# Attention in a decoder step: page numbers kept in registers, four slots for the near masks, and another way to spread the inverse sums

## The chip, the cores and the metric

The kernel runs on one core of one Trainium2 chip. The metric is the time of one execution on the device in microseconds (us). The runs shown of the kernel before took 3438.68, 3438.88 and 3434.42 us, with a median of 3438.68 us. The profile comes from one more execution.

A core has five engines that run instructions of their own queues in order: TensorE (PE, matrix products), VectorE (DVE), ScalarE (ACT), GpSimd (POOL) and SyncE (SP, which here only starts transfers). They wait for each other on semaphores.

## The reference

One inference step of a small decoder with two layers (`DEPTH = 2`): layer 0 has sparse attention (8 heads of 64) and retention side by side, layer 1 a Mamba-2 mixer, and each has an MLP behind it. There are two groups of tokens: a prompt of 1024 tokens, and 8 samples of one token each, with a past of 1024 tokens in pages of 128. The change lies in layer 0's attention.

```python
def sparse_attend(q, kg, vg, idx, tpos, rel_bias):
    dist = tpos[None, :, None] - idx
    bias = jnp.moveaxis(rel_bias[t5_bucket(dist)], -1, 2).astype(jnp.float32)
    logits = jnp.einsum('bqhd,bqkhd->bqhk', q, kg).astype(jnp.float32) * (DH_A ** -0.5) + bias
    logits = jnp.where((dist >= 0)[:, :, None, :], logits, -jnp.inf)
    p = jax.nn.softmax(logits, axis=-1).astype(vg.dtype)
    return jnp.einsum('bqhk,bqkhd->bqhd', p, vg)

# prompt: for each block of QBLK = 128 queries
idx = indexer_topk(iqb, iwb, ik, tpos, k_sel)            # 256 of the keys so far
att = sparse_attend(qb, k[bi, idx], v[bi, idx], idx, tpos, rel_bias)

# samples (even_mixer_sample): keys and values are looked up in pages
page = page_table[bi, pidx // PAGE_SIZE]                 # (8 samples, 8 pages each)
kg = jnp.where(in_past, ck[page, off], k[bi, nidx])
vg = jnp.where(in_past, cv[page, off], v[bi, nidx])
att = sparse_attend(q, kg, vg, idx, pos, rel_bias)
```

## The kernel before

Layer 0's mixer is a sequence of stages. In the profiled execution they are: projection of the tokens and choice of the 256 keys (to about 485 us), the samples' softmax and the storing of k and v (485 to 514), attention of the prompt together with the samples' weighing of values (514 to 708, the function `attend`), and retention. A stage begins when all engines are done with the one before.

**Attention.** The prompt is handled in 8 blocks `i` of 128 queries. Block `i` sees the first `L = (i + 1) * 128` keys. Within a block the 8 heads `h` follow each other, so there are 64 steps `n`. Not chosen and future keys are masked: `scores` holds 1 for them, which `scale_mask` (L1841, POOL) turns into a large negative number. The relative bias matters only for the last 256 keys; POOL adds it to the mask's last 256 columns in `near_mask` (L1851), once for each step, into one of two slots. For one head:

1. PE: `dot_pair` (L1881 to L1893) computes the logits of a pair of heads `q`, 64 rows each, in pieces of 512 columns, into PSUM banks 0 to 3. Before the pair it waits until DVE has read all logits of the pair before (`s_log`).
2. DVE: the far part (L1955) adds the mask to all but the last 256 columns, the near part (L1960) adds the near mask to those; both also give the row maximum. They signal `s_far` and `s_log`. The far part exists from block 2 on. Both wait for the near mask of their step.
3. ACT: the exponential, with its row sum (`s_prob`).
4. PE: transposes of the probabilities, 128 columns each, into PSUM banks 4 and 5 in turn (L1903, `s_turned`), which ACT copies to SBUF (L2004, `s_pt`).
5. PE: the values of a pair weighed with the transposed probabilities into bank 6 (L1915).

For each block, once, the sums must divide the result. Bank 6 holds attention with head and head size on rows (four groups of 128) and queries on columns, while the sums have queries on rows. So:

1. DVE `inverse`: reciprocals `rden` of the 8 row sums (128 x 8).
2. POOL `inverse_rows` (L1856): copies each reciprocal to 64 columns, into `att` (128 x 512), at the second head of the next block.
3. PE `spread_inverse` (L1924): four transposes of that, waited for with `s_rows`, after the second head's own transposes.
4. ACT copies the result to `spread`; DVE `scale_rows` (L1973) multiplies bank 6 with it into `att`.
5. ACT rounds `att` to a high part (L2016, at head 4), and POOL `low` (L1861, at head 5) subtracts it from `att`, which gives the low part. Both go to the output projection, which works with high and low parts.

**Samples.** The values of 8 samples lie in 64 pages of 256 KB. They come in 16 halves `m` of four pages, into a ring of 6 halves (`place`): two in the weight buffers `w_loaded_sb` and `w_high_sb`, four in unused parts of `act_high_sb` and `act_low_sb`. `values_pe` weighs two halves after each of the first two pairs and one after each of the next twelve, each after a wait for its pages (L1516). ACT starts halves 0 to 2, SP the others: halves 3 and 4 in the stage before, among the stores of k and v, and the rest at the head of `attend`, followed by retention's first loads. A half is loaded by `load_pages` (L1331 to L1336):

```python
with eng.Fori(0, self.HALF) as j:
    page = eng.value_load(self.B.pages[0:1, bass.ds(j + m * self.HALF, 1)], min_val=0, max_val=NPOOL - 1)
    eng.dma_start(place[:, bass.ds(j, 1), :],
                  self.B.i[cache][0][bass.ds(page, 1)]...).then_inc(sem, 16)
```

This is a loop of the engine with four passes: it reads the page's number from the table in SBUF into a register (L1334) and starts one transfer (L1335). The key pages are loaded in the same way during the projection, by SP, on whose queue the projection's weights stand as well; POOL multiplies them with the queries (L1368) and DVE sums the products (L1374).

The order of the work is written out by hand: each engine's instructions stand in the order of its function's loops, and nothing else sets it.

## Time and profile before

| | us |
|---|---|
| runs shown: median (lowest to highest) | 3438.68 (3434.42 to 3438.88) |
| profiled execution, its own time | 3435.92 |
| profiled execution, span | 3434.4 |
| PE busy in the span | 3250.5 (95%) |
| DVE, ACT, POOL busy in the span | 1527.5, 1143.6, 1210.8 |
| attention stage | 514 to 708.4 |

The span is the time from the first to the last instruction of the profile; the execution's own time is 1.5 us longer. Attention is 5.7% of the span. PE runs at one of two clock levels, 1.2 and 2.4 GHz; the granted clock of a stretch is given as a share of full speed, so that 0.50 is all of it at the lower level and 1.00 all of it at the higher. In timelines a bracket at a row's end gives the idle time of the engine before it and the engine, tile and line that ended it; `SPq` is SP's own queue, where no computing takes place. In this profile the span's start is zero.

### The profile page before, as it was taken

How to read it: one execution, taken by the hardware profiler on the slowest of the kernel's cores; microseconds unless marked ns; L12 is line 12 of the kernel's file. 1: busy time of each engine (PE TensorE's matmuls, PEld its weight loads, DVE VectorE, ACT ScalarE, POOL GpSimd, SP SyncE). 2: the span in 40 equal slices, each digit the busy share in tenths (PEclk: the TensorE clock that was granted, in tenths of full speed). 3: DMA queues.
4: the chain of work that ended last, by engine and by line, in shares of the span. 5: the costliest groups of instructions: out<-in, count | busy, mean ns of one | idle time of the engine just before them, and what ended most of it. 6: DMA issues, size and time to landing. Idle time of an engine off the chain costs nothing. (4 is left out here: it accounts for less than half of the span.)

```text
span 3434.4 us, 57106 instructions
## 1 busy us (share of the span) xinstructions
PE 3250.5 (95%) x20508; PEld 3062.1 (89%) x20508; DVE 1527.5 (44%) x2685; ACT 1143.6 (33%) x2133; POOL 1210.8 (35%) x898
## 2 busy tenths in 40 slices
PE   7889988888999999999999999999899999999998
PEld 7569974567999999999899999998889999999998
DVE  3799983523221212122556777667742212122122
ACT  3512214532321313132445554545542312222122
POOL 2206844411322221213355555666453221212222
PEclk9989988968999999999999999999999999999999
DMA  4218646022311111112222322222431111111111
GB/s 135 54 31 139 195 172 194 18 79 88 45 49 43 49 45 47 49 43 75 61 84 80 100 94 91 82 86 70 150 134 47 49 44 48 49 43 49 43 49 68
DMA packets 344005, 263.87 MB, mean 77 GB/s; under 512 B 52134, under 2 KB 308150, under 8 KB 341910
## 3 DMA queue, kind: packets, MB, share of 16 engines
q1 hardware_dynamic: 327926, 232.18, 23.2%
q0 software_dynamic: 8192, 19.13, 1.6%
q10 hardware_dynamic: 7776, 11.09, 1.5%
q8 instruction: 68, 1.11, 0.1%
q14 instruction: 43, 0.35, 0.0%
HBM read 219.43 MB, written 44.76 MB: 77 GB/s over the span
## 5 line engine op out<-in xcount | busy, mean ns | idle before, releaser
L234 POOL TENSOR_TENSOR w_low_sb<-w_loaded_sb,w_high_sb 128x1024 fp32r<-128x1024 f32 (+1 forms) x278 | 567.9, 2050 | 1551.3 <-ACT w_high_sb L226 1533.4
L252 PE MATMUL psum<-act_high_sb,w_high_sb 128*128 128x344 f32 (+1 forms) x2400 | 769.4, 321 | 10.0 <-PEq L985 4.0
L252 PE MATMUL psum<-act_low_sb,w_high_sb 128*128 128x344 f32 (+1 forms) x2400 | 767.7, 320 | 0.0
L252 PE MATMUL psum<-act_high_sb,w_low_sb 128*128 128x344 f32 (+1 forms) x2400 | 767.5, 320 | 0.0
L252 PE MATMUL psum<-second_high_sb,w_high_sb 128*128 128x344 f32 x1728 | 553.3, 320 | 0.5 <-PEq L2369 0.5
L252 PE MATMUL psum<-second_low_sb,w_high_sb 128*128 128x344 f32 x1728 | 551.9, 319 | 0.0
L252 PE MATMUL psum<-second_high_sb,w_low_sb 128*128 128x344 f32 x1728 | 551.9, 319 | 0.0
L252 PEld LDWEIGHTS psum<-act_high_sb,w_high_sb 128*128 128x128 f32 (+1 forms) x2400 | 450.5, 188 | 11.3 <-issue 10.0
L252 PEld LDWEIGHTS psum<-act_high_sb,w_low_sb 128*128 128x128 f32 (+1 forms) x2400 | 451.0, 188 | 0.4
L252 PEld LDWEIGHTS psum<-act_low_sb,w_high_sb 128*128 128x128 f32 (+1 forms) x2400 | 450.6, 188 | 0.3
L226 ACT CAST w_high_sb<-w_loaded_sb 128x1024 fp32r<-128x1024 f32 (+1 forms) x230 | 239.5, 1043 | 523.1 <-PE psum L252 496.2
L2970 PE MATMUL psum<-act_high_sb,w_high_sb 128*128 128x344 f32 x1104 | 369.1, 334 | 12.5 <-POOL w_low_sb L234 10.7
L756 DVE TENSOR_TENSOR x_sb<-x_sb,psum 128x344 f32 (+1 forms) x192 | 98.4, 513 | 600.7 <-PE psum L252 600.7
L2970 PE MATMUL psum<-act_high_sb,w_low_sb 128*128 128x344 f32 x1104 | 354.0, 321 | 0.0
L2970 PE MATMUL psum<-act_low_sb,w_high_sb 128*128 128x344 f32 x1104 | 353.7, 320 | 0.0
L252 PEld LDWEIGHTS psum<-second_high_sb,w_high_sb 128*128 128x128 f32 x1728 | 324.5, 188 | 0.8 <-issue 0.8
L252 PEld LDWEIGHTS psum<-second_high_sb,w_low_sb 128*128 128x128 f32 x1728 | 324.8, 188 | 0.0
L252 PEld LDWEIGHTS psum<-second_low_sb,w_high_sb 128*128 128x128 f32 x1728 | 324.5, 188 | 0.0
L688 ACT ACTIVATE relu_square_sb<-relu_sb 128x344 f32<-128x344 f32 x192 | 94.5, 492 | 448.0 <-DVE relu_sb L741 448.0
L741 DVE SCALAR_TENSOR_TENSOR relu_sb<-psum,rstd_sb 128x344 f32<-128x344 f32 x192 | 99.2, 516 | 295.5 <-PE psum L252 271.0
L2970 PEld LDWEIGHTS psum<-act_high_sb,w_high_sb 128*128 128x128 f32 x1104 | 208.9, 189 | 23.0 <-issue 21.9
L2970 PEld LDWEIGHTS psum<-act_low_sb,w_high_sb 128*128 128x128 f32 x1104 | 208.7, 189 | 2.6 <-issue 1.7
(441 smaller groups left out, 4828.9 us busy)
## 6 DMA issues: line engine op xcount, KB each, us to landing
w_loaded_sb<-in_w_up SPq DMA_DIRECT2D x64, 512.0 KB, 4.1
w_loaded_sb<-in_w_down SPq DMA_DIRECT2D x64, 512.0 KB, 4.2
w_loaded_sb<-in_w_in_odd SPq DMA_DIRECT2D x48, 512.0 KB, 3.9
key_pages_sb<-in_cache_k SPq DMA_DIRECT2D x64, 256.0 KB, 2.8
ecay_sum_spread_sb<-decay_sum_scratch SPq DMA_DIRECT2D x8, 2048.0 KB, 9.8
w_loaded_sb<-in_w_in_even SPq DMA_DIRECT2D x28, 512.0 KB, 4.0
gated_scratch<-gated_sb POOLq DMA_DIRECT2D x8, 1032.0 KB, 4.4
ample_ssm_state_sb<-in_state_ssm SPq DMA_DIRECT2D x64, 128.0 KB, 6.9
```

What stands on the lines that cost most here:

```text
L226: self.nc.scalar.copy(self.wh[:, par, :, 0:width], self.wf[:, par, :, 0:width]).then_inc(self.s_w_high, 1)
L234: ins = self.nc.gpsimd.tensor_tensor(self.wl[:, par, k, 0:width], self.wf[:, par, k, 0:width], self.wh[:, par, k, 0:width].bitcast(F32), A ...
L252: ins = nc.tensor.matmul(out, w[:, par, k, 0:width], a[:, k, cols], start=n == 0, stop=n == 3 * KT - 1)
L688: nc.scalar.activation(self.sq[:, s, :], self.relu[:, s, :], ACT.Square).then_inc(self.s_square, 1)
L741: nc.vector.scalar_tensor_tensor(out=self.relu[:, s, :], in0=B.tile(self.par(e), t), scalar=0.0, in1=self.norm.rstd[:, tcols(t)], op0=ALU.max,
L756: nc.vector.tensor_tensor(xs, xs, B.tile(self.par(e), t), ALU.add).then_inc(B.s_tile_free, 1)
L2970: ins = nc.tensor.matmul(B.psum[:, t, 0:TT], w[:, par(e), k, :], a[:, k, tcols(t)], start=m == 0, stop=m == 3 * KT - 1)
```

## The change

The change has five parts.

1. **Page numbers.** `load_pages` is written out as four steps in place of the engine's loop. A new function `number` reads the table; on SP the number of a page from the 20th on is kept in a register of its own after its first read, which is that for the key page, and the value page's load uses the register (44 registers). The places of the ring become tensors of their own at the same addresses.
2. **Near masks and low part.** There are four slots for near masks, so POOL waits for the near part four steps before (not two). The low part of block `i - 1` moves from head 5 to head 7 of block `i`. The last block's low part goes from POOL to DVE.
3. **Spread by products.** POOL's `inverse_rows` goes. PE multiplies each head's reciprocals, read 64 times over as the 64 columns of the stationary side, with the unit matrix: eight products, each giving 64 rows of 128 queries. PE waits for DVE's reciprocals directly. As `att` is no longer used for the copy, DVE's `scale_rows` now waits for POOL's low part of the block before (`s_lo`), and the next reciprocals wait until PE is done with the last ones.
4. **First 512 columns early.** In blocks 5 to 7 and for all pairs of a block but the first, the products of the first 512 columns wait for the far part of the pair before, in place of its near part (`s_far` counts heads from block 2 on, so the number waited for is `2 * q - 2 * HA`). Those of the other columns wait as before.
5. The tensor `inverse_rows_or_att_sb` is called `att_sb`, and the new slots may reach 2048 bytes into `sample_mask_bias_sb`, which was last used in the stage before.

```diff
--- before.py
+++ after.py
@@ -1286,6 +1286,7 @@
+    KEPT = 20
 
...
@@ -1330,10 +1336,18 @@
 
     def load_pages(self, eng, cache, place, m, sem):
 
-        with eng.Fori(0, self.HALF) as j:
-            page = eng.value_load(self.B.pages[0:1, bass.ds(j + m * self.HALF, 1)], min_val=0, max_val=NPOOL - 1)
-            eng.dma_start(place[:, bass.ds(j, 1), :],
+        for j in range(self.HALF):
+            page = self.number(eng, m * self.HALF + j)
+            eng.dma_start(place[:, j:j + 1, :],
                           self.B.i[cache][0][bass.ds(page, 1)].rearrange("o p h d -> p o (h d)")).then_inc(sem, 16)
+
+    def number(self, eng, p):
+
+        if eng is not self.B.nc.sync or p < self.KEPT:
+            return eng.value_load(self.B.pages[0:1, p:p + 1], min_val=0, max_val=NPOOL - 1)
+        if p not in self.kept:
+            self.kept[p] = eng.value_load(self.B.pages[0:1, p:p + 1], min_val=0, max_val=NPOOL - 1)
+        return self.kept[p]
 
@@ -1776,21 +1783,23 @@
...
+    NEAR = 4
     first = B.take("first_blocks_mask_sb", [P, 2 * P])
-    near = B.take("near_mask_sb", [P, 2, 2 * P])
+    near = B.take("near_mask_sb", [P, NEAR, 2 * P])
+
-    att = B.take("inverse_rows_or_att_sb", [P, 512])
+    att = B.take("att_sb", [P, 512])
-    assert B.top <= (B.end - 6400) // 64 * 64, B.top
+    assert B.top <= (B.end - 6400) // 64 * 64 + 4 * NS * PAGES * HA, B.top
...
@@ -1846,15 +1855,10 @@
                 w = min(L, 2 * P)
                 if h == 0:
                     pool.wait_ge(s_mask, max(2, i + 1))
-                if n >= 2:
-                    pool.wait_ge(s_log, n - 1)
-                nc.gpsimd.tensor_tensor(near[:, n % 2, 0:w], mask(i)[:, L - w:L], B.bias[:, h, 2 * P - w:2 * P],
+                if n >= NEAR:
+                    pool.wait_ge(s_log, n - NEAR + 1)
+                nc.gpsimd.tensor_tensor(near[:, n % NEAR, 0:w], mask(i)[:, L - w:L], B.bias[:, h, 2 * P - w:2 * P],
                                         ALU.add).then_inc(s_near, 1)
-
-            def inverse_rows(i):
-                pool.wait_ge(s_rden, i + 1)
-                nc.gpsimd.tensor_copy(att[:].rearrange("p (h d) -> p h d", h=HA),
-                                      rden[:].unsqueeze(2).to_broadcast([P, HA, DH])).then_inc(s_rows, 1)
 
@@ -1866,26 +1870,28 @@
             for n in range(N):
                 i, h = seq[n]
                 near_mask(n)
-                if h == 1 and i >= 1:
-                    inverse_rows(i - 1)
                 if h == 3 and 1 <= i < NBLK - 1:
                     scale_mask(i + 1)
-                if h == 5 and i >= 1:
+                if h == HA - 1 and i >= 1:
                     low(i - 1)
-            inverse_rows(NBLK - 1)
-            low(NBLK - 1)
 
         @block.tensor
         def _(pe):
             def dot_pair(q):
                 i = seq[2 * q][0]
                 L = width(i)
+                early = L - 2 * P >= 512 and q % PAIRS
                 if q >= 1:
-                    pe.wait_ge(s_log, 2 * q)
+                    if early:
+                        pe.wait_ge(s_far, 2 * q - 2 * HA)
+                    else:
+                        pe.wait_ge(s_log, 2 * q)
                 if i == 4 and q % PAIRS == 0:
                     pe.wait_ge(smp.s_colk, NS - 1)
                 for c in range(0, L, 512):
                     w = min(512, L - c)
+                    if c and early:
+                        pe.wait_ge(s_log, 2 * q)
                     for e in range(2):
                         h = seq[2 * q + e][1]
                         r = slice(64 * e, 64 * e + 64)
@@ -1918,10 +1924,12 @@
 
             def spread_inverse(i):
                 k = spread_place[i]
-                pe.wait_ge(s_rows, i + 1)
+                pe.wait_ge(s_rden, i + 1)
                 pe.wait_ge(s_pt, k - 1)
-                for j in range(4):
-                    ins = nc.tensor.transpose(B.psum[:, turn_bank(k), j * P:(j + 1) * P], att[:, j * P:(j + 1) * P], B.ident[:])
+                for h in range(HA):
+                    e, c = 64 * (h % 2), h // 2 * P
+                    ins = nc.tensor.matmul(B.psum[e:e + 64, turn_bank(k), c:c + P],
+                                           rden[:, h:h + 1].to_broadcast([P, DH]), B.ident[:], start=True, stop=True)
                 ins.then_inc(s_turned, 1)
 
             dot_pair(0)
@@ -1957,19 +1965,21 @@
                                                    accum_out=mx[:, n % 3, 0:1]).then_inc(s_far, 1)
                     dve.wait_ge(s_far, n + 1 - 2 * HA)
                     start = mx[:, n % 3, 0:1]
-                nc.vector.tensor_tensor_reduce(out=logit[:, n % 3, far:L], in0=ps[:, far:L], in1=near[:, n % 2, 0:w],
+                nc.vector.tensor_tensor_reduce(out=logit[:, n % 3, far:L], in0=ps[:, far:L], in1=near[:, n % NEAR, 0:w],
                                                scale=-DH ** -0.5, scalar=start, op0=ALU.add, op1=ALU.min,
                                                accum_out=mx[:, n % 3, 1:2]).then_inc(s_log, 1)
 
             def inverse(i):
                 dve.wait_ge(s_prob, HA * (i + 1))
                 if i >= 1:
-                    dve.wait_ge(s_rows, i)
+                    dve.wait_ge(s_turned, spread_place[i - 1] + 1)
                 nc.vector.reciprocal(rden[:], total[:, i % 2, :]).then_inc(s_rden, 1)
 
             def scale_rows(i):
                 dve.wait_ge(s_pv, PAIRS * (i + 1))
                 dve.wait_ge(s_pt, spread_place[i] + 1)
+                if i >= 1:
+                    dve.wait_ge(s_lo, i)
                 nc.vector.tensor_tensor(att[:], B.psum[:, OUT, :], spread[:], ALU.mult).then_inc(s_o, 1)
 
             for n in range(N):
@@ -1983,6 +1993,9 @@
                     rotary.dve(dve, n // 2)
             inverse(NBLK - 1)
             scale_rows(NBLK - 1)
+            dve.wait_ge(s_hi, NBLK)
+            nc.vector.tensor_tensor(B.hl[:, 0:4, SEQ - P:SEQ], att[:].rearrange("p (k c) -> p k c", k=4),
+                                    B.hh[:, 0:4, SEQ - P:SEQ].bitcast(F32), ALU.subtract).then_inc(s_lo, 1)
 
         @block.scalar
         def _(act):
```

How this moves instructions, in three places. First SP's queue, at the first half of value pages in `attend` (`ISA` are register and address steps), before:

```order
L1333 UNCONDITIONAL_BRANCH [waits value_pages_weighed_118]
L1333 ISA
L1334 TENSOR_LOAD page_table_sb_338
L1334 ISA x2
L1335 ISA
L1335 DMA act_high_sb_57<-in_cache_v 128x512
L1333 REGISTER_ALU
L1333 COMPARE_AND_BRANCH
L1738 DMA rotated_sb<-retention_scratch 128x4x1032 [waits value_pages_weighed_118]
```

and after, where this is one half and the start of the next:

```order
L1341 ISA [waits value_pages_weighed_118]
L1341 DMA value_pages_sb<-in_cache_v 128x512
L1341 ISA
L1341 DMA value_pages_sb<-in_cache_v 128x512
L1341 ISA
L1341 DMA value_pages_sb<-in_cache_v 128x512
L1341 ISA
L1341 DMA value_pages_sb<-in_cache_v 128x512
L1341 ISA [waits value_pages_weighed_118]
```

The branch, the loop's step and the read of the table are gone, and a page has two instructions.

Then POOL's queue in the last two blocks (L1851 and L1860 are the near masks, L1841 and L1850 the scaling of the next block's mask, L1856 the copy of the reciprocals, L1861 and L1865 the low part), before:

```order
L1841 TENSOR_SCALAR scores_sb_343<-scores_sb_343 128x1024
L1851 TENSOR_TENSOR near_mask_sb_3978<-scores_sb_343,bias_sb_3524 128x256 [waits logits_177] x2
L1861 TENSOR_TENSOR act_low_sb_58<-inverse_rows_or_att_sb_3982,act_high_sb_57 128x4x128 [waits att_high_185]
L1851 TENSOR_TENSOR near_mask_sb_3978<-scores_sb_343,bias_sb_3524 128x256 [waits logits_177] x2
L1851 TENSOR_TENSOR near_mask_sb_3978<-scores_sb_343,bias_sb_3524 128x256 [waits logits_177,mask_scaled_173]
L1851 TENSOR_TENSOR near_mask_sb_3978<-scores_sb_343,bias_sb_3524 128x256 [waits logits_177]
L1856 COPY inverse_rows_or_att_sb_3982<-prob_sum_inverse_sb_3981 128x512 [waits sum_inverse_182]
L1851 TENSOR_TENSOR near_mask_sb_3978<-scores_sb_343,bias_sb_3524 128x256 [waits logits_177] x4
L1861 TENSOR_TENSOR act_low_sb_58<-inverse_rows_or_att_sb_3982,act_high_sb_57 128x4x128 [waits att_high_185]
L1851 TENSOR_TENSOR near_mask_sb_3978<-scores_sb_343,bias_sb_3524 128x256 [waits logits_177] x2
L1856 COPY inverse_rows_or_att_sb_3982<-prob_sum_inverse_sb_3981 128x512 [waits sum_inverse_182]
```

and after:

```order
L1860 TENSOR_TENSOR near_mask_sb_4445<-scores_sb_343,bias_sb_3880 128x256 [waits logits_177,mask_scaled_173]
L1860 TENSOR_TENSOR near_mask_sb_4445<-scores_sb_343,bias_sb_3880 128x256 [waits logits_177] x3
L1850 TENSOR_SCALAR scores_sb_343<-scores_sb_343 128x1024
L1860 TENSOR_TENSOR near_mask_sb_4445<-scores_sb_343,bias_sb_3880 128x256 [waits logits_177] x4
L1865 TENSOR_TENSOR act_low_sb_58<-att_sb_4449,act_high_sb_57 128x4x128 [waits att_high_184]
L1860 TENSOR_TENSOR near_mask_sb_4445<-scores_sb_343,bias_sb_3880 128x256 [waits logits_177,mask_scaled_173]
L1860 TENSOR_TENSOR near_mask_sb_4445<-scores_sb_343,bias_sb_3880 128x256 [waits logits_177] x7
L1865 TENSOR_TENSOR act_low_sb_58<-att_sb_4449,act_high_sb_57 128x4x128 [waits att_high_184]
```

The copies are gone, and the low part stands behind all eight near masks of a block; the last one is no longer on POOL.

Last PE's queue in block 7, around the spread of block 6 and the pair behind it (L1903 and L1909 are transposes, L1892 and L1898 the logit products), before:

```order
L1903 MATMUL psum<-ident_sb_49,qkv_sb_1841 128x128 [waits probs_copied_180,probs_178]
L1903 MATMUL psum<-ident_sb_49,qkv_sb_1841 128x128 x3
L1903 MATMUL psum<-ident_sb_49,qkv_sb_1841 128x128 [waits probs_copied_180]
L1903 MATMUL psum<-ident_sb_49,qkv_sb_1841 128x128 x3
L1924 MATMUL psum<-ident_sb_49,inverse_rows_or_att_sb_3982 128x128 [waits probs_copied_180,inverse_rows_183]
L1924 MATMUL psum<-ident_sb_49,inverse_rows_or_att_sb_3982 128x128 x3
L1892 MATMUL psum<-qkv_sb_1841 128x512 [waits logits_177]
L1892 MATMUL psum<-qkv_sb_1841 128x512 x3
L1903 MATMUL psum<-ident_sb_49,qkv_sb_1841 128x128 [waits probs_copied_180,probs_178]
L1903 MATMUL psum<-ident_sb_49,qkv_sb_1841 128x128 x3
```

and after:

```order
L1909 MATMUL psum<-ident_sb_49,qkv_sb_1841 128x128 [waits probs_copied_180,probs_178]
L1909 MATMUL psum<-ident_sb_49,qkv_sb_1841 128x128 x3
L1909 MATMUL psum<-ident_sb_49,qkv_sb_1841 128x128 [waits probs_copied_180]
L1909 MATMUL psum<-ident_sb_49,qkv_sb_1841 128x128 x3
L1931 MATMUL psum<-ident_sb_49,prob_sum_inverse_sb_4448 64x128 [waits probs_copied_180,sum_inverse_182]
L1931 MATMUL psum<-ident_sb_49,prob_sum_inverse_sb_4448 64x128 x7
L1898 MATMUL psum<-qkv_sb_1841 128x512 [waits far_logits_176]
L1898 MATMUL psum<-qkv_sb_1841 128x512
L1898 MATMUL psum<-qkv_sb_1841 128x512 [waits logits_177]
L1898 MATMUL psum<-qkv_sb_1841 128x512
L1909 MATMUL psum<-ident_sb_49,qkv_sb_1841 128x128 [waits probs_copied_180,probs_178]
L1909 MATMUL psum<-ident_sb_49,qkv_sb_1841 128x128 x3
```

The pair's four products fall into two that wait for the far logits and two that wait for all, and the spread has eight products of 64 x 128 where it had four of 128 x 128.

## Rows read from the trace of the kernel before

**Rows 1.** Window: us; PE, PEld, DVE, ACT, POOL busy; PE clock, DMA share, GB/s.
```profile
514.00:708.40 194.40, 160.67 (x1281) 99.82 (x1281) 84.68 (x272) 101.33 (x241) 77.32 (x88) 0.90 0.37 107
```

**Rows 2.** Waits in that stage: us in total, times, longest us.
```profile
DVE qkv_sb L1955 <- POOL near_mask_sb L1851: 21.2, 6, 3.7
...
PE psum L1516 <- DMA act_high_sb<-in_cache_v: 3.3, 2, 1.9
...
PE psum L1516 <- DMA w_high_sb<-in_cache_v: 2.6, 1, 2.6
...
PE psum L1516 <- DMA w_loaded_sb<-in_cache_v: 1.0, 1, 1.0
```

**Rows 3.** SP's queue, timeline: start us, us, value-page loads.
```profile
522.37 4.79 SPq L1335 DMA_DIRECT2D w_loaded_sb<-in_cache_v  x4
528.27 4.79 SPq L1335 DMA_DIRECT2D w_high_sb<-in_cache_v  x4
```

**Rows 4.** SP, one instruction: ns min/median/max, first and last start.
```profile
L1334 SPq TENSOR_LOAD <-page_table_sb x116: 262/268/1092, 283.1 to 581.0; - x116
...
L1335 SPq DMA_DIRECT2D act_low_sb<-in_cache_v x16: 345/351/390, 501.3 to 557.8; - x16
```

**Rows 5.** Windows, columns as Rows 1: one clean pair, three slow stretches.
```profile
558.12:562.71 4.59, 4.59 (x39) 2.69 (x39) 2.11 (x10) 3.38 (x9) 1.48 (x2) 1.00 0.69 181
...
543.40:558.00 14.60, 12.75 (x66) 6.35 (x62) 3.67 (x19) 4.11 (x11) 4.20 (x5) 0.65 0.65 172
...
571.00:582.00 11.00, 9.08 (x52) 5.56 (x52) 0.93 (x4) 2.67 (x7) 3.25 (x4) 0.69 0.61 166
...
653.80:660.00 6.20, 6.14 (x31) 3.70 (x33) 3.36 (x9) 2.78 (x5) 1.65 (x1) 0.54 0.00 0
```

**Rows 6.** DVE, timeline: far part of head 6, block 4.
```profile
613.58 0.56 DVE L1955 CUSTOM_DVE_ANT_0 qkv_sb<-psum,scores_sb 128x384 f32<-128x384 f32 x1 [3.65 <-POOL near_mask_sb L1851]
```

**Rows 7.** PE, timeline: the products around four waits behind DVE or ACT.
```profile
610.08 1.35 PE L1892 MATMUL psum<-qkv_sb 64*128 64x512 f32 x8
...
615.73 1.56 PE L1892 MATMUL psum<-qkv_sb 64*128 64x512 f32 x8 [1.67 <-DVE minus_row_max_sb L1960]
...
640.16 1.77 PE L1892 MATMUL psum<-qkv_sb 64*128 64x512 f32 x8 [1.28 <-DVE minus_row_max_sb L1960]
...
667.93 1.99 PE L1892 MATMUL psum<-qkv_sb 64*128 64x512 f32 x8 [0.90 <-DVE minus_row_max_sb L1960]
...
697.32 1.06 PE L1903 MATMUL psum<-ident_sb,qkv_sb 128*128 128x128 f32 x8 [0.93 <-ACT probs_turned_sb L2004]
```

**Rows 8.** PE, timeline, block 7: spread, late products, weighing of values.
```profile
679.45 0.63 PE L1924 MATMUL psum<-ident_sb,erse_rows_or_att_sb 128*128 128x128 f32 x4 [0.39 <-ACT qkv_sb L2004]
682.95 3.36 PE L1892 MATMUL psum<-qkv_sb 64*128 64x512 f32 x8 [2.87 <-DVE minus_row_max_sb L1960]
...
693.39 1.97 PE L1915 MATMUL psum<-probs_turned_sb,v_rows_sb 128*64 128x128 f32 x32
```

**Rows 9.** DVE, timeline: far part and near part of head 3, block 7.
```profile
681.41 0.95 DVE L1955 CUSTOM_DVE_ANT_0 qkv_sb<-psum,scores_sb 128x768 f32<-128x768 f32 x1
...
682.40 0.48 DVE L1960 CUSTOM_DVE_ANT_0 qkv_sb<-psum,near_mask_sb,minus_row_max_sb 128x256 f32<-128x256 f32 x1
```

**Rows 10.** POOL, timeline: the last low part.
```profile
706.78 1.26 POOL L1861 TENSOR_TENSOR act_low_sb<-erse_rows_or_att_sb,act_high_sb 128x512 fp32r<-128x512 f32 x1 [7.07 <-ACT act_high_sb L2016]
```

**Rows 11.** SP's queue, timeline: the stage's last load.
```profile
698.00 0.39 SPq L1746 DMA_DIRECT2D halves_or_values_sb<-retention_scratch  x1
```

**Rows 12.** DVE, timeline: two sums of the projection, a k copy.
```profile
299.97 1.22 DVE L1374 TENSOR_REDUCE sample_logits_sb<-key_pages_sb 128x32 f32<-128x1024 f32 x1 [4.48 <-POOL key_pages_sb L1368]
...
483.39 1.22 DVE L1374 TENSOR_REDUCE sample_logits_sb<-key_pages_sb 128x32 f32<-128x1024 f32 x1
...
497.35 0.69 DVE L1707 COPY k_rows_sb<-psum 128x512 f32<-128x512 f32 x1 [0.92 <-DMA out_k_prompt<-k_rows_sb]
```

**Rows 13.** PE, timeline: projection products behind a weight's low part.
```profile
302.32 0.42 PE L252 MATMUL psum<-act_high_sb,w_high_sb 128*128 128x344 f32 x1 [2.27 <-POOL w_low_sb L234]
```

More of the change, by code:

```diff
@@ L1323, in take_ring @@
         B = self.B
+        self.kept = {}
+        slots = [B.w_base + 4 * 2 * KT * P * a for a in range(2)]
+        slots += [base + 4 * (4 * TOK + a * self.HALF * 512) for base in (B.act_base, B.hl_base) for a in range(2)]
+        self.slots = [B.nc.alloc_sbuf_tensor_at(f"value_pages_{r}_sb", [P, self.HALF, 512], F32, offset=o)
+                      for r, o in enumerate(slots)]
         self.kp = B.take("key_pages_sb", [P, self.KRING, self.HALF, 512])
@@ L1479, in place @@
     def place(self, m):
-        B, r = self.B, m % self.VRING
-        if r < 2:
-            a = (B.wf[:], B.wh[:].bitcast(F32))[r]
-            return a.rearrange("p a k m -> p (a k m)").rearrange("p (j c) -> p j c", c=512)
-        a = (B.hh, B.hl)[(r - 2) // 2][:, 4:8, :].bitcast(F32).rearrange("p k c -> p (k c)")
-        c0 = (r - 2) % 2 * self.HALF * 512
-        return a[:, c0:c0 + self.HALF * 512].rearrange("p (j c) -> p j c", c=512)
+        return self.slots[m % self.VRING][:]
     def load_values(self, eng, m):
@@ L1790, in attend @@
     OUT = 6
-    (s_mask, s_near, s_dot, s_far, s_log, s_prob, s_turned, s_pt, s_pv, s_rden, s_rows, s_o, s_hi, s_lo) = (
+    (s_mask, s_near, s_dot, s_far, s_log, s_prob, s_turned, s_pt, s_pv, s_rden, s_o, s_hi, s_lo) = (
         B.sem(x) for x in ("mask_scaled", "near_mask", "logit_products", "far_logits", "logits", "probs", "probs_turned",
-                           "probs_copied", "values_weighted", "sum_inverse", "inverse_rows", "att", "att_high", "att_low"))
+                           "probs_copied", "values_weighted", "sum_inverse", "att", "att_high", "att_low"))
     width = lambda i: (i + 1) * P
```

## The prediction

> **What bounds the kernel now.** I read the windows first, stage by stage, then the waits of the stage that the change is in, then that stage's timelines on SP, PE, DVE and POOL. Outside attention PE sets the pace; over 194.4 us of attention it is busy for 160.7 us, at a mean clock of 0.90, and no other engine is busier than 101 us [rows 1]. So PE is the nearest thing to a bound there, and what can be won is its idle time (194.4 - 160.7 = 33.7 us) and the time lost at the lower of its two clock levels. The reader should look for who releases PE, not for who is busy. Three sorts of release matter. PE waits three kinds of value pages [rows 2]. DVE waits POOL's near masks and, one wait later, PE waits DVE [rows 2, 6, 7]. And once a block DVE waits for the spread inverse, and PE for DVE [rows 8].
>
> **Value pages (page numbers in registers).** SP starts a half of four pages every 5.90 us (528.27 - 522.37) although the four starts take 4.79 us and one DMA instruction 0.35 us; the rest is the table read (0.27 us), register work and the loop [rows 3, 4]. A pair of heads with a half in it and no such wait took PE 4.59 us, from its first product to the next pair's [rows 5], so SP falls behind and PE waits 3.3 + 2.6 + 1.0 = 6.9 us [rows 2]. The stall is paid twice. In the two stretches around these waits the granted clock is 0.65 and 0.69, that is most of the time at the 1.2 GHz level, each after PE had stood idle. PE is busy 12.75 of 14.60 us and 9.08 of 11.00 us there; at the mean clock, busy time lost against full speed is 12.75 x 0.35 + 9.08 x 0.31 = 4.5 + 2.8 = 7.3 us [rows 5]. In the new order a half that the ring has room for is four pairs of a register step and a DMA instruction, some 4 x 0.5 = 2 us, well under 4.6. What is late next: the transfers. At 0.65 of the engines' time they moved 172 GB/s, so 265 GB/s at all of it, and a half of 1.05 MB takes 4.0 us; that is under 4.6 us too, but not by much, and the ring is six halves deep. PE's wait for the spread in block 2 grows back by an estimated 0.8 us, since the slow clock had covered it. I take 6.9 + 7.3 - 0.8 = 13.4 us gained. Bounds: 0 (transfers keep the old pace) to 14.2.
>
> The Trainium skill (DMA: Bandwidth & Descriptors, "Bandwidth") gives 341 GB/s for a transfer of 1 MB and 425 at best: by that a half would take 3.1 us, and the term would be the same. The row's 265 GB/s is what I use.
>
> **Near masks and low part.** Before, POOL's low part of block i-1 stands two near masks before the end of block i and waits for ACT's high part, which comes late; DVE then waits for near mask 6, 3.65 us in block 4 [rows 6]. PE had the products of that head done at 610.08 + 1.35 = 611.43, so DVE could have started 2.1 us earlier [rows 6, 7]. With four slots the masks are made up to four heads ahead, and the low part stands behind all eight, with the whole of the next pair to hide in. PE's idle time behind this is 1.67, 1.28, 0.90 us in blocks 4 to 6 and 0.93 us in block 7 (there by way of ACT): 4.8 us gained [rows 7]. In blocks 1 to 3 the same wait cost PE nothing that a row shows. Each price is limited by PE's idle time, not by DVE's 3.65 us, because PE's own queue is late next. Bounds 2 to 5. The new wait that this brings, scaling the rows of block i only after the low part of block i-1, is met half a block before. The added wait in POOL's queue has eight mask starts behind it and none is due.
>
> **Spread by products.** The copy on POOL (once per block) goes; PE waited for ACT's copies, not for it [rows 8], so this gives nothing. Four transposes, 0.63 us, become eight fp32 products with 64 columns of weights, and these come two per product: 16 records. The nearest row is the weighing of values, same shape (128 x 64 by 128), 32 records in 1.97 us [rows 8]. With an estimated 0.27 us for the last one to end it is (1.97 - 0.27) / 32 = 0.053 us each. 16 x 0.053 + 0.27 = 1.12 us, so +0.49 us, eight times, on the chain that ends with DVE's scaling: a loss of 3.9 us. Low bound 0.2 us each; high bound, if the two column halves don't run side by side and each record takes twice as long, 16 x 0.107 + 0.27 = 1.98, +1.35 us each or 10.8 us.
>
> One rule speaks against it: the Trainium skill (TensorEngine Tiling (Array Packing), "Key Properties") says that changing the tiling mode drains the engine, and the products change it where transposes did not. The rows show such a change without a visible gap, since weighing follows transposes at once; a drain is at most the 0.27 us of one product's end, so the sum would be 2.2 us worse by the rule at its full price.
>
> **First 512 columns early.** In blocks 5 to 7 three pairs of four may begin when the far part of the head before is done. It matters where PE waits for DVE, which is the pair after the spread: the far part ends at 681.41 + 0.95 = 682.36 and the near part at 682.89 [rows 9], and PE starts at 682.95 after 2.87 us idle [rows 8]. The first two products of about 0.5 us each cover the near part, so the pair is done 0.53 us earlier: 3 x 0.53 = 1.6 us. Bounds 0 to 1.6; elsewhere PE comes late to the wait and nothing is gained.
>
> **End of the stage.** The last low part goes from POOL, 1.26 us [rows 10], to DVE, where the nearest operation on 512 columns (the k copy) takes 0.69 us [rows 12]: 0.6 us gained. SP's last load, 2 MB, is started at 698.00 [rows 11] and at the 265 GB/s above lands some 8 us later, at 706, and the new chain still ends after it: old end 706.78 + 1.26 = 708.04, less 0.6, plus the spread's 0.5. The load, 2 us ahead of it, is what would be late next.
>
> **Before attention.** The loop goes for all pages, but the table is still read once for each. Of a page's 4.79 / 4 = 1.20 us, 0.27 is the read, 0.35 the DMA instruction, and 0.58 register work and loop [rows 3, 4]; I take a quarter of that, 0.15 us, for the loop. In projection DVE waited 4.48 us for the first key half, PE 2.27 us for a weight that SP had queued behind these keys, and DVE's last sum there ends at 484.61 with nothing to wait for, so the stage ends with DVE's chain [rows 12, 13]. The first four pages then start 0.6 us earlier, and as much again without the entry into the loop (the longest table read took 1.09 us against 0.27 [rows 4]): I take 1.3 us off both waits (0 to 2.3). In the stage after it SP's k stores stand behind a half of value pages, and DVE waits 0.92 us and once again about half as long for them: 0.8 us (0 to 1.2) [rows 12]. The register copies on SP cost nothing that anyone waits for.
>
> **The sum.** 13.4 + 4.8 + 1.6 + 0.6 + 1.3 + 0.8 - 3.9 = 18.6 us. The profiled execution took 3435.92 us (its span 3434.4 and 1.5 around it), 2.8 us below the median of the runs shown, 3438.68. From its own time the sum gives 3417.3; from the median 3420.1. I forecast 3419, between them and nearer to the median.
>
> **Rivals.**
> - The clock stays low. The stalls go, but one or both stretches at the lower level come back behind other waits (the spread leaves over 1.4 us of idle time in a block): 7.3 us less, 3426. For it: in block 7 the level falls behind a spread wait alone, which stays, and 653.8 to 660 has 0.54 [rows 5]. Against it: 558 to 571 would run as now without a stall. 0.20.
> - The clock gains. The spread waits of blocks 5 to 7 get shorter by 0.5 us and the low stretches behind them vanish. One of them costs 6.14 x 0.46 = 2.8 us [rows 5]; three together an estimated 6: 3413. The idle time is still over 2 us, so 0.12.
> - Transfers bind. The pages land no faster than in the old rows (4 us a half at best against pairs of 4.6): 13.4 us less, 5.2 gained, 3432. 0.07.
> - The masks don't do what they are for: POOL, which waits for s_log and ACT as before, delivers them at the same moment, and the early columns find nothing idle. 6.4 us less, 3425. The order speaks against it. 0.06.
> - Slower: the spread. If its products go one by one and each record pays its full latency and an unhidden weight load, as much as the 3.36 / 8 = 0.42 us that a record of 512 columns took at the lower level [rows 8], it takes 16 x 0.42 = 6.7 us, +6.1 us eight times, 49 us against the 3.9 in the sum: 3464. The change turns slower once a spread takes over 0.63 + 22.5 / 8 = 3.4 us. The weighing of values shows an eighth of that price per record, so 0.03.
> - The forecast itself: 0.52.
>
> **Range and chances.** 3410 to 3430 takes in the clock either way, the masks' failure, and the spread up to its high bound (+6.9 us); transfers bound and the slower case lie outside. What a measurement can tell from no change is 0.2%, 6.9 us: same is 3432 to 3446. Transfers bound falls on its edge. Faster 0.90, same 0.07, slower 0.03.
>
> **What would show it.** Value-page DMAs of a half 2 us long in SP's timeline, no wait of PE for them, and a clock near 1.00 from 543 to 582. No wait of DVE for near masks but the first. A spread of about 1.1 us. PE's idle time in blocks 4 to 7 down to the spread waits. Attention some 16.5 us shorter and the stages before it some 2. It is wrong if attention gives back less than 10 us, if retention behind it changes by over 2 us, or if a spread takes over 1.5 us.

## The result and the profile after

| | before | changed |
|---|---|---|
| runs beside each other, median | 3438.68 us | 3418.99 us |
| profiled execution, own time | 3435.92 us | 3418.30 us |
| span | 3434.4 us | 3416.5 us |
| attention, first product to retention's first product | 514.12 to 708.40 | 514.53 to 690.97 |

The changed kernel takes 0.9949 of the time before, 95% interval 0.9937 to 0.9961: 19.7 us between the medians and 17.6 between the profiled executions. The forecast was 3419 us.

Windows of the changed kernel, columns as [rows 1]: attention, then block 2, block 3 (each from its first logit product to the next block's), and the time in which SP starts its last 44 value pages.

```profile
514.53:690.97 176.44, 156.10 (x1376) 99.32 (x1377) 85.25 (x273) 101.38 (x241) 71.05 (x79) 0.94 0.36 118
543.76:561.78 18.02, 16.82 (x147) 8.98 (x143) 8.07 (x38) 9.43 (x26) 8.87 (x12) 1.00 0.40 139
561.78:581.53 19.75, 18.41 (x162) 10.57 (x158) 8.71 (x38) 10.42 (x25) 8.12 (x10) 1.00 0.14 45
514.60:549.10 34.50, 32.22 (x235) 15.45 (x235) 10.85 (x52) 14.40 (x54) 17.92 (x27) 0.88 1.01 352
```

The same stretches of the kernel before, which [rows 5] showed only in part:

```profile
514.12:708.40 194.28, 160.67 (x1281) 99.80 (x1281) 84.68 (x272) 101.33 (x241) 77.29 (x88) 0.90 0.37 107
543.42:567.42 24.00, 20.99 (x135) 10.75 (x131) 8.07 (x38) 9.66 (x26) 9.02 (x11) 0.79 0.65 177
567.42:592.74 25.32, 21.11 (x150) 12.24 (x147) 8.69 (x38) 10.25 (x24) 8.75 (x11) 0.87 0.53 151
```

Attention is 17.84 us shorter, and 5.98 + 5.57 = 11.55 us of it lie in blocks 2 and 3. Their clock is 1.00, with 0.79 and 0.87 before. From the starts of the blocks in PE's timeline, the rest is 1.30, 1.51, 0.79 and 1.97 us in blocks 4 to 7, 0.65 us behind the last spread, and 0.07 us in blocks 0 and 1. One of the stalls that went, 1.91 us, lay in block 1 (PE's timeline before, 542.42), but the clock was low for longer at the stage's start.

The waits in attention, answering to [rows 2]; those of PE for value pages have no row any more.

```profile
PE psum L1898 <- DVE minus_row_max_sb L1968: 7.3, 5, 2.5
PE psum L1898 <- DVE minus_row_max_sb L1963: 6.6, 3, 2.3
...
DVE qkv_sb L1968 <- POOL near_mask_sb L1860: 3.9, 1, 3.9
```

Only the first near mask is waited for (21.2 us in six waits before for the far parts, [rows 2]). Of PE's waits behind DVE those behind the spread are left; three are now ended by a far part (L1963). In block 7 the timelines of PE and DVE show this, answering to [rows 8 to 10]:

```profile
664.65 1.09 PE L1931 MATMUL psum<-ident_sb,prob_sum_inverse_sb 128*64 128x128 f32 x16 [0.38 <-ACT qkv_sb L2017]
668.08 1.99 PE L1898 MATMUL psum<-qkv_sb 64*128 64x512 f32 x8 [2.33 <-DVE minus_row_max_sb L1963]
```
```profile
667.06 0.95 DVE L1963 CUSTOM_DVE_ANT_0 qkv_sb<-psum,scores_sb 128x768 f32<-128x768 f32 x1
...
668.06 0.48 DVE L1968 CUSTOM_DVE_ANT_0 qkv_sb<-psum,near_mask_sb,minus_row_max_sb 128x256 f32<-128x256 f32 x1
...
689.96 0.69 DVE L1997 TENSOR_TENSOR act_low_sb<-att_sb,act_high_sb 128x512 fp32r<-128x512 f32 x1 [0.68 <-ACT act_high_sb L2029]
```

The spread has 16 records in 1.09 us (forecast 1.12), the products start as the far part ends, 0.54 us earlier than in [rows 8], and the last low part takes DVE 0.69 us (forecast 0.69). The eight products of the pair run at full clock here, 1.99 us and not 3.36.

SP's queue: the first key half, the 44 value pages of attention and one half of them alone, answering to [rows 3]; then SP's waits in that time, and the window 520 to 540.

```profile
283.29 3.67 SPq L1341 DMA_DIRECT2D key_pages_sb<-in_cache_k  x4
...
514.61 34.46 SPq L1341 DMA_DIRECT2D value_pages_sb<-in_cache_v  x44
...
529.46 1.91 SPq L1341 DMA_DIRECT2D value_pages_sb<-in_cache_v  x4
```
```profile
SPq L1341 <- PE psum L1523: 8.2, 6, 2.0
```
```profile
520.00:540.00 20.00, 19.18 (x152) 8.74 (x144) 6.32 (x27) 8.23 (x31) 6.92 (x10) 0.92 1.05 383
```

With a table read a half's four starts take 3.67 us, not 4.79 (loop). Without reads they take 1.91 us, and the next half can follow after 2.1 us, as forecast. All 44 pages take longer, 34.46 / 11 = 3.1 us a half, because SP waits 8.2 us of that time for PE to free a place in the ring. The DMA engines are full there, with a share of 1.05 at 383 GB/s, which gives 2.7 us a half (1.05 MB / 383). Both are under the 4.6 us that PE needs.

In the stage before attention, DVE's first copy and its waits for k stores:

```profile
484.82 0.68 DVE L1714 COPY sample_qkv_rows_sb<-psum 8x512 f32<-8x512 f32 x1 [1.24 <-PE psum L1694]
...
497.63 0.69 DVE L1714 COPY k_rows_sb<-psum 128x512 f32<-128x512 f32 x1 [1.89 <-DMA out_k_prompt<-k_rows_sb]
498.98 0.69 DVE L1714 COPY k_rows_sb<-psum 128x512 f32<-128x512 f32 x1 [0.66 <-DMA out_k_prompt<-k_rows_sb]
500.30 0.69 DVE L1714 COPY k_rows_sb<-psum 128x512 f32<-128x512 f32 x1 [0.63 <-DMA out_k_prompt<-k_rows_sb]
```

The first copy stood at 485.85 before, so the projection won 1.03 us; the waits were 0.92 and 0.52 us [rows 12] and are longer now. The stage lost 1.44 us, and attention starts 0.4 us later than before.

### The profile page after: what moved, and what is told of

Same layout as the page of the kernel before. It is cut to its first block and busy times, and to the rows that moved or that the text cites. A ratio compares the mean times of both kernels' runs of the same rounds, so it can differ in the third digit from the quotient of the medians.

```text
span 3416.5 us, 56741 instructions
## 1 busy us (share of the span) xinstructions
PE 3243.2 (95%) x20604; PEld 3060.4 (90%) x20604; DVE 1527.9 (45%) x2686; ACT 1143.8 (33%) x2132; POOL 1206.0 (35%) x889
```

## The experiments

All times are medians of runs beside the kernel before, ratios are to it. "Lost" is what PE's busy time loses to the lower clock level, counted as for the forecast (busy time multiplied by one less the granted clock, over attention in steps of 1 us): 18.4 us before, 9.9 us in the changed kernel.

**Page numbers alone.** The kernel before with this part of the diff only.

> The kernel before with the page numbers alone (written-out loads, numbers kept in registers). Theory (stalls and clock): PE's three waits for value pages and both stretches at the lower clock level behind them go; blocks 2 and 3 together take 38 to 39 us where they took 49.3 (before, first product of block 2 at 543.42 to that of block 4 at 592.74), blocks 4 to 7 change by under 1 us, and the storing stage before attention takes about 1.4 us longer while the projection ends 1 us earlier: the profiled execution near 3435.9 - 12 = 3424. Rival (the clock follows the spread's idle time): the lower level comes back in blocks 2 and 3 and only the 6.9 us of stalls are won: 3429. Rival (the near slots did part of it): blocks 2 and 3 take over 41 us.

3422.62 us, 0.9954 (0.9940 to 0.9968). Attention, block 2, block 3:

```profile
513.62:693.38 179.76, 152.44 (x1281) 95.75 (x1281) 84.60 (x272) 101.16 (x241) 77.29 (x88) 0.94 0.35 115
542.20:559.63 17.43, 16.22 (x134) 8.57 (x130) 8.07 (x39) 9.36 (x27) 9.08 (x12) 1.00 0.43 147
559.63:579.17 19.54, 17.91 (x151) 10.19 (x147) 8.79 (x39) 10.54 (x26) 8.99 (x12) 1.00 0.16 49
```

Blocks 2 and 3 take 36.97 us, 12.35 less than before, and lost time is 9.8 us: the theory of stalls and clock, a little better than its 38 to 39. In these two blocks lay 5.0 us of the stalls and 8.5 us of lost time; both are gone, and the spread wait in block 2 grew by 0.6 us. Attention is 14.5 us shorter in all, blocks 4 to 7 1.4 us of it (under 1 expected). The projection ended 2.5 us earlier (1 expected), and the stage behind it took 2.0 us longer (1.4).

**Loads written out, the table read each time.** The same with `KEPT = 64`.

> The kernel before with written-out page loads that read the table each time (no numbers kept). What does a page cost on SP then: in the changed kernel a key page with its table read takes 3.60 / 4 = 0.90 us against 1.20 us in the loop. Theory (SP's pace is what counts, and 4.59 us a pair is its threshold): a half takes 4 x 0.90 = 3.6 us and less than a pair, so PE's waits for value pages go as they did with the numbers in registers; blocks 2 and 3 together take 37.4 us as in that run, and the time is within 2 us of its 3422.6. Rival (the registers matter): SP reaches the ring's end later and at least one wait of over 1 us stays, with the lower clock level behind it: 3428.

3423.95 us, 0.9960 (0.9948 to 0.9973), attention 179.78 us, no wait of PE for pages. The kept registers bring nothing that can be told: it is the engine's loop whose going does it. A half of value pages in SP's queue:

```profile
535.18 3.59 SPq L1341 DMA_DIRECT2D value_pages_sb<-in_cache_v  x4
```

The time of a row x4 holds three steps from page to page and the last DMA instruction (0.35 us before, 0.33 here). So a page takes (4.79 - 0.35) / 3 = 1.48 us in the loop, (3.59 - 0.33) / 3 = 1.09 us written out with the read, and (1.91 - 0.33) / 3 = 0.53 us with the number kept: the loop costs 0.39 us a page, the read with its register work 0.56. At 1.09 us the next half starts 4.37 us later (539.55), not 3.6 as expected, and that is only just under PE's 4.6.

**Four slots and the low part at head 7 alone.**

> The kernel before with four near-mask slots and the low part at head 7 alone. Theory: DVE's waits for near masks go but the first, and blocks 4 to 7 (615.73 - 592.74 and so on, to the end of the last spread) take some 4.8 us less, about 1.7, 1.3 and 0.9 us in blocks 4 to 6; blocks 2 and 3 stay as they are: near 3431. Rival (the early columns did it): the waits of PE behind DVE in blocks 4 to 6 stay, 3436.

3431.58 us, 0.9984 (0.9975 to 0.9993). Attention, and block 4, which took 22.99 us:

```profile
515.36:704.64 189.28, 159.48 (x1281) 99.33 (x1281) 84.69 (x272) 101.30 (x241) 75.12 (x88) 0.90 0.36 110
595.17:616.41 21.24, 18.06 (x156) 13.22 (x155) 10.00 (x39) 13.09 (x31) 9.46 (x11) 0.92 0.76 212
```

5.0 us shorter, with the waits of 1.67, 1.28 and 0.90 us gone from PE: the theory. But the total agrees in part by luck. The fourth wait, 0.93 us in block 7, kept 0.39 us; blocks 0 to 3 took 1.2 us more, where the value pages still stall PE; and block 7 lost the stretch at the lower clock level behind its spread (1.7 us), though the wait there was as long as before:

```profile
681.37 1.99 PE L1895 MATMUL psum<-qkv_sb 64*128 64x512 f32 x8 [2.87 <-DVE minus_row_max_sb L1963]
```

**Early columns off.**

```diff
-                early = L - 2 * P >= 512 and q % PAIRS
+                early = False
```

> The changed kernel without the early wait for the first 512 columns. Theory: PE's wait behind the spread of blocks 5 to 7 goes from 2.06, 2.19, 2.33 us back to about 2.60, 2.74, 2.87 us, and nothing else changes: attention 1.6 us longer, 3419.9. Rival (the clock): the 0.5 us decide whether the clock falls behind the spread of block 7, where it stayed at 1.00 with the change and was 0.67 before; then block 7 loses another 1.5 us: 3421.4.

3422.25 us, 0.9956 (0.9944 to 0.9969). Attention took 179.77 us, 3.3 more. The waits behind the spread were 2.59, 2.73 and 2.86 us, as expected (1.6 us in all), and a stretch of lost time stood in block 7 again, 1.7 us. The total is that of the rival, but that the early columns keep the clock up in block 7 is not shown. Without them and with the 2.87 us wait the clock stayed up there in the kernel of the masks alone. With them and with the short wait it fell in "The fifth half later", a kernel below with the same order in attention on PE and DVE:

```profile
666.45 3.67 PE L1896 MATMUL psum<-qkv_sb 64*128 64x512 f32 x8 [2.33 <-DVE minus_row_max_sb L1961]
```

What the early columns are worth by themselves is the 1.6 us of waits.

**Transposes back.** The changed kernel with `inverse_rows` and the four transposes.

> The changed kernel with the spread as before (POOL's copies of the reciprocals, four transposes); the rest as changed. Theory (the products lie on the chain): each of the eight spreads takes 0.63 in place of 1.09 us and attention gets 8 x 0.46 = 3.7 us shorter: 3414.6 from the profiled execution's 3418.3. Rival (the direct wait for the reciprocals pays for the products): PE then waits for POOL's copy in some blocks, and the time is within 1 us of 3418.3. Rival (the cleared copy gives the clock): the low part of a block now stands between copies, and DVE waits for it.

3413.19 us, 0.9933 (0.9921 to 0.9946).

```profile
513.99:684.43 170.44, 149.93 (x1280) 94.73 (x1281) 85.33 (x273) 101.18 (x241) 73.79 (x87) 0.95 0.36 122
```

6.0 us shorter than with the products: the 3.7 us of the theory, and 2.5 us less lost time (7.4 us). The products are a loss, as forecast. The lost time can't be put down to them, since the next run, with twice the products, has less of it.

**Products twice.**

```diff
-                for h in range(HA):
+                for h in list(range(HA)) * 2:
```

> The changed kernel with each of the spread's eight products made twice (the second overwrites the first with the same numbers). Theory (0.053 us a record, all of it on the chain through ACT's copy and DVE's scaling to PE's next products): a spread takes 1.09 + 16 x 0.053 = 1.94 us, attention 8 x 0.85 = 6.8 us longer: 3425.1 from the profiled 3418.3, and PE's idle time behind the spread stays at its 2.1 to 2.5 us. Rival (partly hidden): PE's idle time behind the spread shrinks by what the spread grows, and the time is under 3421.

3420.34 us, 0.9955 (0.9943 to 0.9967). PE around the spread in block 6, of the kernel with the products twice and of the changed one:

```profile
635.53 1.97 PE L1931 MATMUL psum<-ident_sb,prob_sum_inverse_sb 128*64 128x128 f32 x32 [0.49 <-ACT probs_turned_sb L2017]
639.69 1.77 PE L1898 MATMUL psum<-qkv_sb 64*128 64x512 f32 x8 [2.19 <-DVE minus_row_max_sb L1963]
```
```profile
636.47 1.09 PE L1931 MATMUL psum<-ident_sb,prob_sum_inverse_sb 128*64 128x128 f32 x16 [0.49 <-ACT probs_turned_sb L2017]
639.76 3.36 PE L1898 MATMUL psum<-qkv_sb 64*128 64x512 f32 x8 [2.19 <-DVE minus_row_max_sb L1963]
```

Each spread took 0.88 us more and the wait behind it stayed, 7.0 us in all, as the theory says. But attention took 177.94 us, only 1.5 more: lost time was 3.9 us, not 9.9. The low stretches of blocks 4 to 6 are gone, and one of 1.6 us in block 7 is new. The expected total was wrong by the clock. The time is the rival's (under 3421), its reason is not.

**Both once more**, for one profile each, to tell a rule from chance.

> The changed kernel once more, for one profile. The busy time lost at the lower clock level in attention was 9.95 us there, in four stretches: at its start and behind the spreads of blocks 4, 5 and 6 (counted by when they happen), none behind that of block 7. Theory (the stretches hang on where the idle time falls): the same four come again, within 1.5 us in all. Rival (they come and go from one execution to the next): one of them is missing or one in block 7 is there.

> The kernel with the spread's products made twice once more, for one profile. There each spread took 1.97 us and its idle time behind stayed at 2.06 to 2.46 us, so its chain was 7.0 us longer, but attention only 1.5 us longer, since only one stretch at the lower clock level was left behind the spreads (lost busy time 3.9 us in all against 9.95). Theory (PE's work in front of the idle time keeps the clock): the stretches in blocks 4 to 6 are missing again, lost busy time under 6 us. Rival (chance): they are there, lost busy time about 10 us and attention over 183 us.

3418.53 and 3419.74 us, one run each.

```profile
513.54:689.58 176.04, 155.70 (x1376) 98.81 (x1377) 85.23 (x273) 101.31 (x241) 71.03 (x79) 0.94 0.36 118
```
```profile
513.38:691.31 177.93, 157.58 (x1505) 102.81 (x1505) 84.99 (x273) 101.25 (x241) 71.06 (x79) 0.97 0.36 117
```

The stretches came again in the same blocks: lost 9.4 and 3.8 us. So for one kernel they are no chance of a single execution, in two profiles of each. But a small edit of the loads ahead of attention moves them, as the next two runs show (lost 10.2 and 7.0 us), so a pair of profiles doesn't tell which part of a change took one away.

**The fifth half later.** The changed kernel with `AHEAD = 4` and without the load between the k stores.

> The changed kernel with the fifth half of value pages started at the head of attention, not between the last k stores of the stage before. Theory (the transfers are full in that stage): DVE's waits for k stores there, 1.89 + 0.66 + 0.63 us in the changed kernel, shrink by about a half, and the stage, from DVE's first copy (484.82) to attention's first product (514.53), takes 1 to 1.5 us less; PE gets no wait for value pages. Rival (SP's order): the stores that DVE waits for were all started before that half, and nothing changes. Rival: the half then lands late, and PE waits over 1 us in attention's third pair: attention longer by as much, and by 2 us where the clock falls.

3419.50 us, 0.9945 (0.9933 to 0.9958). From DVE's first copy (483.54) to attention's first product (513.97) it took 30.43 us, no less than the 29.71 of the changed kernel. My theory fell: that half is not what the stores wait for. Attention took 177.07 us, with 10.2 us lost: 1.5 us of it in block 6, where the changed kernel had 3.1, and 1.6 us in block 7, where it had none.

**ACT's halves in the loop.** The changed kernel, with SP's loads alone written out.

> The changed kernel with ACT's three halves of value pages in the engine's loop, as before; SP's loads as changed. Theory (ACT's twelve page loads, started in a shorter time, keep the k stores waiting in the stage before attention): DVE's waits for k stores go from 1.89 + 0.66 + 0.63 us back to about 0.9 + 0.5, and from DVE's first copy to attention's first product it takes 28.3 to 28.8 us, not 29.7. Rival (it is the bytes, 9.7 MB in 29 us at up to 390 GB/s, not who starts them): no difference over 0.5 us.

3413.13 us, one run. DVE's copies in that stage:

```profile
482.09 0.68 DVE L1720 COPY sample_qkv_rows_sb<-psum 8x512 f32<-8x512 f32 x1 [1.24 <-PE psum L1700]
...
493.76 0.69 DVE L1720 COPY k_rows_sb<-psum 128x512 f32<-128x512 f32 x1 [0.68 <-DMA out_k_prompt<-k_rows_sb]
495.08 0.69 DVE L1720 COPY k_rows_sb<-psum 128x512 f32<-128x512 f32 x1 [0.62 <-DMA out_k_prompt<-k_rows_sb]
```

The waits are 0.68 and 0.62 us, and the stage takes 510.67 - 482.09 = 28.58 us, as expected if ACT's twelve pages, started in 12.31 us with the change and 17.69 here, are what the k stores wait behind. That isn't shown, though. In the kernel with the masks alone, whose ACT has the loop too, DVE waited 2.44 and 0.33 us and the stage took 29.46 us. Over all profiles the stage took 28.3 to 29.5 us in the three with ACT's loop and 29.7 to 30.4 in the eleven without, so the direction is likely and the price is open. The DMA engines were no fuller with the change either (share 0.87 from 485 to 514, 0.91 before). The rest of the gain (a start 1.5 us earlier than in the second profile of the changed kernel, 2 us less in attention) was not expected, and one run doesn't settle it.

**Scaling behind the fourth head's logits**, with the transposes back.

```diff
-                if n % HA == 2 and n >= HA:
+                if n % HA == 3 and n >= HA:
                     scale_rows(n // HA - 1)
```

> The changed kernel with the transposes back, and DVE's scaling of the rows behind the logits of the block's fourth head, not its third. PE's idle time behind each spread (2.5 us in block 4, 2.1 to 2.3 in blocks 5 to 7, 12.4 us over all blocks) is DVE standing in front of the scaling while the logits of the fourth head are ready to be made. Theory: that idle time goes, and with it the lower clock level behind it (5.1 us of busy time lost in three stretches): attention 12 + 5 = 17 us shorter than with the transposes alone, 153 us, and 3396. Rival (the weighing is next): PE then waits for the scaling in front of the next block's first weighing, since bank 6 must be free, and half of it stays: 3405. Rival (no change): the early columns already took what was to be had.

3396.69 us, 0.9877 (0.9863 to 0.9892): the best version, 22 us under the changed kernel's median. Attention, then PE and DVE around a spread, block 6:

```profile
513.32:667.24 153.92, 145.60 (x1280) 92.02 (x1281) 84.29 (x273) 100.53 (x241) 71.65 (x87) 0.97 0.41 135
```
```profile
621.57 0.63 PE L1940 MATMUL psum<-ident_sb,att_sb 128*128 128x128 f32 x4 [0.49 <-ACT probs_turned_sb L2023]
622.12 1.77 PE L1908 MATMUL psum<-qkv_sb 64*128 64x512 f32 x8
```
```profile
619.97 0.48 DVE L1976 CUSTOM_DVE_ANT_0 qkv_sb<-psum,near_mask_sb,minus_row_max_sb 128x256 f32<-128x256 f32 x1
...
622.92 0.69 DVE L1989 TENSOR_TENSOR att_sb<-psum,inverse_spread_sb 128x512 f32<-128x512 f32 x1 [2.46 <-ACT inverse_spread_sb L2031]
```

DVE still waits for the spread, but with all logits made. PE's products follow the spread at once, and the lost time is 3.3 us, all at the stage's start. That is the theory (153 and 3396 expected).

**The same with the products kept.**

> The changed kernel with the scaling of rows behind the logits of the fourth head, and the spread by products kept. With the transposes this gave 3396.7 and attention 153.9 us. Theory (behind the moved scaling a spread costs only PE's time): each of the eight products' spreads adds 0.46 us to PE, 3.7 us in all: attention 157.6, 3400.4, and no idle time of PE behind the spreads. Rival (the later spread makes the weighing of the next block's first pair wait for the scaling): over 159 us. Rival (it is hidden): 154.

3397.97 us, 0.9892 (0.9875 to 0.9908); attention 157.09 us. The products cost 3.2 us of attention, nearly their 3.7, in the one profile; the two medians are not told apart. Expected were 157.6 and 3400.4.

## Why the prediction was right

- **Value pages**, 13.4 us forecast (0 to 14.2). Measured 12.35 us in the two blocks and 14.5 us over attention with this part alone. Both halves of the term were there: the stalls, and the clock (lost time 18.4 to 9.8 us; the mean clock had put the two stretches at 7.3 us, in steps of 1 us they are 8.5). SP's 2 us a half were right. The 265 GB/s worked out from [rows 5] was too low for the transfers: 383 was reached. Kept registers, which the title names first, were not needed. The loop was priced from 4.79 / 4 = 1.20 us a page, but that row holds three steps and not four: a page takes 1.48 us, and the loop, taken at 0.15 us of it, cost 0.39.
- **Near masks and low part**, 4.8 forecast, 5.0 measured alone, in part by luck: the idle time of PE that went was 1.67 + 1.28 + 0.90 + 0.54 = 4.4 us, and the rest is the clock of block 7 against longer early blocks.
- **Spread by products**, 3.9 us lost forecast; 0.46 us each, 3.7 in all. No gap stands in front of the spread in blocks 1 to 3, so the drain that the prediction sets against it did not show. The attention stages differ by 6.0 us, but the 2.5 us of clock in that are not shown to be the products'.
- **Early columns**, 1.6 forecast; the waits shrank by that. The clock stayed up in block 7, one of the three stretches of my rival "the clock gains", but the runs do not tie that to the early columns.
- **End of the stage**, 0.6 forecast, 0.65 measured.
- **Before attention**, 2.1 forecast. The projection won 1.0 us here, and about 2.4 in ten of the eleven other profiles with written-out key loads (first copy at 483.1 to 483.7, and at 482.1 in the last, where both kernels with the loop had 485.9). The 0.8 us for the stage behind it had the wrong sign: it became 1.4 us longer. I had thought of SP's queue alone and passed over ACT's loads, which the same function writes out. The stage is shorter in all three kernels that leave them in the loop, but why and by how much stays open.
- **Sum.** 16.5 us in attention forecast, 17.84 measured; 2.1 ahead of it forecast, -0.4 measured; 18.6 against 17.6 from the profiled execution's own time. The errors of the two parts cancelled in part. Behind attention two more changes nearly cancel. Retention, which I had expected to stay, took 2.7 us less (108.4 us to the output products before, 105.7 after), which is over the 2 us that the prediction names as a sign of being wrong, and 2.3 us were given back behind it (2617.6 us before, 2619.8 after; 2617.3 to 2622.1 over all profiles). So the time agrees better than its parts. Retention in both kernels, columns as [rows 1]:

```profile
708.40:816.82 108.42, 94.35 (x479) 71.08 (x479) 28.24 (x44) 26.11 (x33) 12.37 (x10) 0.63 0.26 83
690.97:796.67 105.70, 91.53 (x479) 68.24 (x479) 28.25 (x44) 26.11 (x33) 12.39 (x10) 0.66 0.26 85
```

PE's idle time there is the same (14.1 and 14.2 us), its busy time is 2.8 us less and its clock 0.66 in place of 0.63: the gain is in the clock. It came back, larger or smaller, in all kernels whose last low part is on DVE (105.2 to 107.7 us; 108.0 to 108.9 in the three others). Why the low stretch lies otherwise there was not tested and stays open.

- **Rivals.** "The clock stays low" fell for blocks 2 and 3. "Transfers bind" is right that they become full, and wrong on the price (2.7 us a half). The slow spread fell: 0.07 us a record.

## What to carry to other kernels

Price a stall twice where a low stretch of PE's clock follows it: in blocks 2 and 3, 5.0 us of stalls went together with 8.5 us of lost time. But do not credit a part of a change with a low stretch from one pair of profiles: here the stretches moved between blocks in kernels whose attention was the same. Then ask why the last wait stays: PE idled behind each spread because DVE stood in its queue in front of work that was ready, and moving one call by one head won 16.5 us over the transposes alone (170.4 to 153.9), nearly as much as the whole change. Where a helper is called from two queues, follow both: it changes the loads of each.

## What was not expected of the hardware

The stretches at the lower clock level came again in a second profile of the same kernel (lost 9.9 and 9.4 us, 3.9 and 3.8 us, in the same blocks), and moved with edits that left attention's order on PE and DVE alone (9.9 to 10.2 and 7.0 us). The idle time just before does not decide: behind 2.87 us of it the eight products in block 7 took 1.99 us in one kernel, behind 2.33 us they took 3.67 us in another. Neither does the work ahead of it: with 1.97 us of products in the place of 1.09 three stretches went and one came, and the transposes, with less work, also left less lost time (7.4 us). The runs show no simple rule. SP takes 1.48 us from page to page in the engine's loop, 1.09 us written out, and 0.53 us with the number in a register.
